# Opening of a one-core hybrid decoder step: the first input products placed between the activation transposes, with scalings, a square, two evictions and a root reordered around them

## What is computed

```python
h = rmsnorm(x, norm_mix[l])
proj = h @ w_in[l]
u = proj[..., :SSM_WIDTH]
zc = proj[..., SSM_WIDTH:SSM_WIDTH + CONV_WIDTH]
gb = proj[..., SSM_WIDTH + CONV_WIDTH:SSM_WIDTH + 2 * CONV_WIDTH]
gc = proj[..., SSM_WIDTH + 2 * CONV_WIDTH:]
...
x = x + mix @ w_out[l]
x = x + moe(hf.reshape(bt * L, D), ...)
```

## Time and profile before

| | us |
|---|---|
| median of 3 runs | 1483.16 (1482.44 to 1484.73) |
| the profiled execution | 1483.9 |
| its span from first to last instruction | 1482.0 |
| PE busy in the span | 1424.6 (96%) |
| DVE busy | 1322.5 (89%) |
| ACT busy | 1029.7 (69%) |
| mean granted TensorE clock | 0.983 |

### The profile page before, as it was taken

One profiled execution on the slowest core, in us unless ns is written; L12 is line 12 of the kernel. 1 busy time (PEld: TensorE's weight loads), 2 busy tenths in 40 slices (PEclk: granted clock), 3 DMA queues, 4 the chain that ended last, 5 costly groups with the idle time before them and its releaser, 6 DMA issues.

```text
span 1482.0 us, 22671 instructions
## 1 busy us (share of the span) xinstructions
PE 1424.6 (96%) x7043; PEld 1137.9 (77%) x7044; DVE 1322.5 (89%) x1751; ACT 1029.7 (69%) x1240; POOL 142.7 (10%) x151
## 2 busy tenths in 40 slices
PE   6999889799999999999999999999999999999993
PEld 5888744477888888888888888888888888888882
DVE  5887566789999999999999999999999999999994
ACT  3010332678888888887888888888888888888773
POOL 8100020100000010000000000000000000100000
PEclk9999999799999999999999999999999999999996
DMA  9510482399999999999999999999999999999953
GB/s 306 67 33 1 157 306 108 109 376 409 374 377 376 377 376 370 372 377 377 372 376 371 373 375 378 369 371 372 369 362 360 375 380 374 370 377 374 371 232 120
DMA packets 85285, 469.42 MB, mean 317 GB/s; under 512 B 17934, under 2 KB 19206, under 8 KB 68360
## 3 DMA queue, kind: packets, MB, share of 16 engines
q1 hardware_dynamic: 73160, 447.86, 75.4%
q0 software_dynamic: 12096, 21.18, 6.4%
HBM read 457.56 MB, written 27.82 MB: 328 GB/s over the span
## 4 chain that ended last, share of the span: by engine, by line
PE 78%; DVE 1%; ACT 1%; DMA 1%; issue 1%; SPq 0%; POOLq 0%; DVEq 0%
PE bank L1751 73%; PE bank L1736 2%; PE bank L1742 2%; PE bank L1758 1%; ACT w_hi L1648 0%; DVE w_lo L1820 0%; DMA token_sums<-ymix,row_cur 0%; DMA x<-token_sums 0%; PE bank L1729 0%; DVE x L1901 0%; DVE ymix L1901 0%; ACT ymix L1686 0%; ACT ring_lo L1710 0%; SPq L1587 0%; DVE cmix L1841 0%
## 5 line engine op out<-in xcount | busy, mean ns | idle before, releaser
L1820 DVE TENSOR_TENSOR w_lo<-ring_lo,w_hi 128x1024 fp32r<-128x1024 f32 x527 | 610.1, 1220 | 26.3 <-ACT w_hi L1648 26.2
L1648 ACT ACTIVATE w_hi<-ring_lo 128x1024 fp32r<-128x1024 f32 x527 | 543.5, 1058 | 86.3 <-PE bank L1751 77.6
L1751 PE MATMUL bank<-w_hi,x_hi 128*128 128x512 f32 x1056 | 332.7, 396 | 1.4 <-DVE w_lo L1820 1.4
L1751 PE MATMUL bank<-w_lo,x_hi 128*128 128x512 f32 x1056 | 326.9, 391 | 0.0
L1751 PE MATMUL bank<-w_hi,x_lo 128*128 128x512 f32 x1056 | 326.3, 390 | 0.0
L1820 DVE TENSOR_TENSOR w_lo<-w_out,w_hi 128x1024 fp32r<-128x1024 f32 x264 | 311.2, 1221 | 11.2 <-ACT w_hi L1648 11.1
L1648 ACT ACTIVATE w_hi<-w_out 128x1024 fp32r<-128x1024 f32 x264 | 268.1, 1054 | 18.2 <-PE bank L1751 18.2
L1751 PEld LDWEIGHTS bank<-w_lo,x_hi 128*128 128x128 f32 x1056 | 198.9, 188 | 42.0
L1751 PEld LDWEIGHTS bank<-w_hi,x_lo 128*128 128x128 f32 x1056 | 198.9, 188 | 42.0
L1751 PEld LDWEIGHTS bank<-w_hi,x_hi 128*128 128x128 f32 x1056 | 193.7, 189 | 38.6 <-DVE w_lo L1820 1.9
L1751 PE MATMUL bank<-w_hi,h_hi 128*128 128x512 f32 x528 | 170.0, 403 | 0.0
(11 more groups left out here) (367 smaller groups left out, 1189.7 us busy)
## 6 DMA issues: line engine op xcount, KB each, us to landing
ring_lo<-in_w_gate_up SPq DMA_DIRECT2D x132, 2048.0 KB, 11.5
w_out<-in_w_down SPq DMA_DIRECT2D x132, 1024.0 KB, 13.8
ring_lo<-in_w_in SPq DMA_DIRECT2D x4, 2048.0 KB, 22.0
w_out<-in_w_out SPq DMA_DIRECT2D x2, 2048.0 KB, 8.9
x<-in_x_prompt SPq DMA_DIRECT2D x6, 512.0 KB, 9.0
bias<-bias_rows SPq DMA_DIRECT2D x132, 3.0 KB
token_sums<-x SPq DMA_DIRECT2D x4, 512.0 KB
ffn_in<-hf SPq DMA_DIRECT2D x4, 512.0 KB, 3.8
```

What stands on the lines that cost most here:

```text
L1648: nc.scalar.activation(high(j), raw(j), ACT.Copy).then_inc(s["w_hi"], 1)
L1751: last = nc.tensor.matmul(bank[b + u][:], v[:, k, :], part(j)[:, u, :], start=(j == 16 and first), stop=(j in (7, 15, UNITS - 1) and part ...
L1820: v.tensor_tensor(low(j), raw(j), high(j).bitcast(F32), ALU.subtract).then_inc(s["w_lo"], 1)
```

## The change

On PE, three plain matmuls with the identity as weights and 512 columns of tile 0 as the moving operand are put at the very start; they write bank 7 and nobody reads the result. Only the first three tiles are transposed ahead of the products. Then the low halves of steps 0 and 1 are done, with the transposes of the last two tiles between them, and then the high halves of step 0 and of step 1. The `arow` transposes still come after the high half of step 0. On ACT, the scalings of tiles 0 and 2 are ahead of the square of tile 4 and the second root. On DVE, the evictions of the first two tiles are ahead of the second variance, the third is ahead of the second refinement, the last two are behind it. `pcol` is copied ahead of all of these.

```diff
@@ scalar @@
         root(0)
         square(3)
+        scale(0)
+        scale(2)
         square(4)
         root(1)
-        for i in (0, 2, 3, 4):
-            scale(i)
+        scale(3)
+        scale(4)
@@ tensor @@
         pe.wait_ge(s["ident"], 1)
+        pe.wait_ge(x_in[0], 32)
+        for q in range(3):
+            nc.tensor.matmul(bank[7][:], ident[:], x[:, 0, 0:512], start=True, stop=True)
         pe.wait_ge(s["prow_in"], 16 * 7)
...
-        for p in range(NT):
+        for p in range(FIRST[0][1]):
             x_transposes(p)
         pe.wait_ge(s["pcol"], 1)
...
             if n == 0:
                 pe.wait_ge(s["hT"], 2 * FIRST[0][1])
+                for n1 in range(2):
+                    for k in range(KD):
+                        nc.tensor.matmul(bank[2 * n1][:, 0:HALF], w_in[:, 0, k, ORDER[n1] * P:(ORDER[n1] + 1) * P], hT[:, k, 0:HALF],
+                                         start=(k == 0), stop=(k == KD - 1))
+                    if n1 == 0:
+                        for p in range(FIRST[0][1], NT):
+                            x_transposes(p)
+                pe.wait_ge(s["hT"], 2 * NT)
+            if n <= 1:
                 for k in range(KD):
-                    nc.tensor.matmul(lo[:, 0:HALF], w_k(k), hT[:, k, 0:HALF], start=(k == 0), stop=(k == KD - 1))
-                pe.wait_ge(s["hT"], 2 * NT)
-                for k in range(KD):
-                    last = nc.tensor.matmul(hi[:, 0:REST], w_k(k), hT[:, k, HALF:TOK], start=(k == 0), stop=(k == KD - 1))
+                    last = nc.tensor.matmul(bank[2 * n + 1][:, 0:REST], w_in[:, 0, k, m * P:(m + 1) * P], hT[:, k, HALF:TOK],
+                                            start=(k == 0), stop=(k == KD - 1))
@@ vector @@
-        for c, (lo, hi) in enumerate(FIRST):
...
+        variance(0)
+        inverse(0)
+        dve.wait_ge(s["rstd"], 1)
+        ts(xs[1], x[:, 1, :], ss[:, NT + 1:NT + 2], ALU.mult).then_inc(s["xs_dve"], 1)
         dve.wait_ge(s["prow_psum"], 1)
         nc.vector.tensor_copy(pcol[:], bank[0][:, 0:PC]).then_inc(s["pcol"], 1)
         dve.wait_ge(s["pcol"], 1)
-        for p in range(NT):
-            take_hT(p)
+        take_hT(0)
+        take_hT(1)
+        variance(1)
+        take_hT(2)
+        inverse(1)
+        take_hT(3)
+        take_hT(4)
```

More of the change, by code:

```diff
@@ L669, in take_hT, with variance, inverse @@
                    pcol[:, NM + 4 * q:NM + 4 * q + 4].unsqueeze(2).to_broadcast([P, 4, n]), ALU.mult).then_inc(s["hT"], 1)
-        for c, (lo, hi) in enumerate(FIRST):
+        def variance(c):
+            lo, hi = FIRST[c]
             dve.wait_ge(s["ss"], hi)
             ts(ss[:, lo:hi], ss[:, lo:hi], 1.0 / D, ALU.mult, EPS, ALU.add).then_inc(s["var"], 1)
+        def inverse(c):
+            lo, hi = FIRST[c]
             dve.wait_ge(s["root"], c + 1)
             refine_rsqrt(nc, done, ss[:, NT + lo:NT + hi], ss[:, 2 * NT + lo:2 * NT + hi], ss[:, lo:hi]).then_inc(s["rstd"], 1)
-            if c == 0:
-                dve.wait_ge(s["rstd"], 1)
-                ts(xs[1], x[:, 1, :], ss[:, NT + 1:NT + 2], ALU.mult).then_inc(s["xs_dve"], 1)
+        variance(0)
+        inverse(0)
+        dve.wait_ge(s["rstd"], 1)
+        ts(xs[1], x[:, 1, :], ss[:, NT + 1:NT + 2], ALU.mult).then_inc(s["xs_dve"], 1)
         dve.wait_ge(s["prow_psum"], 1)
```

## The result

The changed kernel takes 1486.93 us (median of 9 runs, 1486.16 to 1488.27) beside 1483.16 (9 runs, 1481.68 to 1485.13). The ratio is 1.0022, with a 95% interval of 1.0014 to 1.0030: between 2.1 and 4.4 us slower. The forecast was 1486.3, with 3.1 us lost. The profiled execution took 1487.22, its span is 1485.3 in place of 1482.0.

What follows compares the result with a forecast made beforehand. The prediction took TensorE as the bound, its first products waiting on the `w_in` load. Moved transposes 1.55, halves and transitions 0.15 and clock 1.4 summed to 3.1 us, giving 1486.3 us on the median, range 1484.3 to 1487.8.

Steps and rivals of the forecast that it cites:

- The load pins the first product: Opening: the first quarter of `w_in` still lands at 18.4, so PE's products still start at 18.49.
- The moved transposes: Sixteen transposes of tiles 3 and 4 move behind the first eight matmuls, where PE has no gap: 1.55 us lost.
- Halves and transitions: Switching between products and transposes, and doing step 1 as 8 + 8 instead of alternating: an estimated 0.15 us lost.
- The clock: PE's pause before the first product widens to 4.2 us, and the granted clock falls to 0.50: 1.4 us lost.
- the sum (3.1): Total loss forecast for the opening: 1.55 + 0.15 + 1.4 = 3.1 us.
- My rival with a pause of 2.2 us: Before the first product: the clock holds, with the pause free or only 2.2 us; 1484.9 us, chance 0.22.
- the case of the first product before 16.8: Rival at PE's wait before the first product: the load lands earlier, gaining 2.1 against 1.7; 1482.8 us, chance 0.08.
- Opening matmuls cost nothing: Start of PE: the three matmuls take 2.7 to 5.3 us, done by 10.3, ahead of `prow` at 10.63.
- Scalings of tiles 3 and 4 are ready before PE asks: On ACT: scaled by 18.5 and 19.6, before PE asks at 22.1; evictions end by 25.
- DVE behind the opening: DVE's table work starts 6.6 us later, but 10.7 us covers it, so nothing is late.
- The transposes do not hold the clock: Rival before the products: PE counts as standing from 10 to 18.49, costing 1.7 + 1.7 = 3.4 us; 1486.6, chance 0.03.

Runs made afterwards that it cites:

- e6: Changed kernel with POOL's four small b-table loads issued behind its other loads: 1484.93 us, ratio 1.0004 to the kernel before.
- e1: Changed kernel with four more unread matmuls in PE's pause, behind the transposes of the first three tiles: 1485.46 us, ratio 1.0013 to the kernel before.
- e3: Changed kernel without the three opening matmuls: 1487.66 us, ratio 1.0026 to the kernel before.
- e8: Changed kernel with POOL's four b-table loads issued late and two unread matmuls in PE's pause: 1482.39 us, ratio 0.9994 to the kernel before.
- e4: Kernel before with the three opening matmuls alone added: 1484.18 us, ratio 0.9998 to the kernel before.
- e2: Changed kernel with all five tiles transposed ahead of the products again: 1488.07 us, ratio 1.0029 to the kernel before.
- e11: Kernel before with POOL's four b-table loads issued late and five opening matmuls: 1482.80 us, ratio 0.9989 to the kernel before.
- e7: Kernel before with POOL's four b-table loads issued late and the three opening matmuls: 1482.12 us, ratio 0.9996 to the kernel before.
- e5: Kernel before with POOL's four b-table loads issued behind its other loads: 1482.54 us, ratio 0.9993 to the kernel before.
- e10: Repeat of e5, the kernel before with POOL's four b-table loads issued late: 1483.55 us, ratio 0.9999 to the kernel before.

## Why the prediction was right, and where not

- **The load pins the first product.** Right: PE's wait of 4.83 us ends on `ring_lo<-in_w_in`, and e6 shows that `hT` for three tiles is there some 3 us earlier (16.64). But I took one execution's landing, 18.4, for fixed. It was 18.4 to 20.3 over the six profiles that left the loads alone. So the forecast of the first product at 18.4 to 18.6 was too narrow.
- **The moved transposes**, 1.55: measured 1.57 in the changed kernel, e1, e3, e6 and e8 alike. That is a reading of traces: no run took this term away by itself.
- **Halves and transitions**, 0.15: measured 0.11.
- **The clock**, 1.4: measured 1.68. The stretch lay wholly on the products; I had let 0.4 us of it fall into the pause. This term was mis-sized by 0.3, and it is the whole difference between the sum (3.1) and the trace (3.36). That the pause causes it is shown by e1, where filling it gave the 3.63 us back. The place of the stretch was partly luck. I took the fall to come 3.7 us after PE stops, from one case. It came 5.1 us after in the changed kernel (14.83 to 19.98), 2.7 in e6 and 2.5 in e3, and where it came before the products, in e3, the term was 2.9.
- **A shorter pause would hold the clock.** My rival with a pause of 2.2 us took that from the pause of 1.00 us. e6 shows a fall after 2.26, at a cost of 1.68. In the case of the first product before 16.8 I had also left the clock's price out: 2.1 against 1.7 would have been 2.1 against 3.4.
- **Opening matmuls cost nothing.** Right (e3, e4). That they give nothing by themselves is right too, but my reason, that the load covers all, is only half of it: in e4 the clock had fallen again before most of the transposes ran.
- **Scalings of tiles 3 and 4 are ready before PE asks.** True of the changed kernel (17.84 against 24.98), and the evictions ended at 27.7, before the high half at 30.21. e2 shows that this is due to the place where PE asks.
- **DVE behind the opening.** Right: its first table operation starts at 34.68 and takes 0.17 us, and PE has no gap from its first product to 156 us.
- **The transposes do not hold the clock** (the rule of the Trainium skill, "TensorE: Matmul & The Clock Gate", Part 4). e11 speaks against it for fp32 transposes: PE did nothing but transposes from 12.6 to 17.3, at 0.12 us each, and the first low half still took 3.63 us (17.82 to 21.45). Counted as standing, PE would have stood there for 5.2 us, longer than the 4.83 after which the clock fell in the changed kernel. In e4 the transposes came with pauses between them, and the clock fell; it then stayed at 0.50 through 6 us of transposes without a pause (14.27 to about 20.3). That does not speak for the rule, since in e3 it stayed there through 5.8 us of products.

What stays open: the medians differ by 3.8 us and the traces account for 3.36. The interval, 2.1 to 4.4, holds both, and I have no second profile of the kernel before that would show where its products usually start. The transposes' 1.57 us rest on traces alone, and why the load landed earliest in the profile of the kernel before is not known.

## What to carry to other kernels

Work that hides under a wait is free there; moving it behind the wait puts all of it on the path, and it pays only if the start moves by more than that work. Before starting early on a part of the data, ask what else may be last (here a DMA that no reordering touched), and how long TensorE will now stand, since pauses of 2.3 to 4.8 us here cost a further 1.7 us, and once 2.9, at half clock. Matmuls that nobody reads can hold the clock, if they leave no long pause up to the real work: with 1.1 and 1.4 us it held (e1, e8), with 1.63 and 1.76 it fell (e4, e7). A wait that ends on a DMA in one profile is no fixed point either: look at the same load in several.

## What the runs showed of the hardware

Beside four loads of 64 KB in 64-byte pieces the core's DMA moved 150 to 220 GB/s for about 4 us in the kernel before (12 to 16), where it moved some 360 right before and after. In e5, with these loads moved behind, it moved 343 to 371 there. The 2 MB load landed 2.8 us earlier on average (mean of 19.5 in six profiles without the edit, 16.7 in seven with it). An earlier landing, though, gains nothing that can be measured when TensorE is just as late (e5, e10).

The clock fell more easily than I had thought: in e4 after pauses of 1.63 and 0.22 us, with the short `prow` transpose between them and tile 1's eight transposes behind, in e6 after 2.26 us. And a fall just ahead of the work cost more than one just behind its start: 2.9 us in e3 against 1.68 in the changed kernel and e6. Two more falls just ahead of work lasted as long as e3's, 6.8 us: in e2 (21.2 to 28.0, work from 21.32) and later in the changed kernel (180.4 to 187.2, work from 181.09). Three cases are no rule, and the cause stays open.
